# Hybrid decoder layer on one core: a different interleaving of block transposes, LayerNorm passes and sums at the start of the second FFN

## The reference, cut to what matters

```python
def trunk_layer(x, ...):
    x = layer_norm(ALPHA * x + 0.5 * swiglu(x, ffn_wi[0], ffn_wo[0]), ln_g[0], ln_b[0])
    ...                      # attention and retention, merged
    x = layer_norm(ALPHA * x + merged @ w_o, ln_g[1], ln_b[1])
    x = layer_norm(ALPHA * x + 0.5 * swiglu(x, ffn_wi[1], ffn_wo[1]), ln_g[2], ln_b[2])

def swiglu(x, wi, wo):
    g, u = jnp.split(x @ wi, 2, axis=-1)
    return (jax.nn.silu(g) * u) @ wo
```

## Time and profile before

| | |
|---|---|
| median of 3 runs | 2407.12 us (2403.64 to 2409.01) |
| the profiled execution | 2408.45 us, its span 2406.6 us |
| TensorE busy | 2375.1 us (99% of the span) |
| VectorE, ScalarE, GpSimd busy | 1673.8, 911.1, 211.9 us |
| mean granted TensorE clock | 0.996 |

### The profile page before, as it was taken

One profiled execution on the slowest core, in us unless ns is written; L12 is line 12 of the kernel. 1 busy time (PEld: TensorE's weight loads), 2 busy tenths in 40 slices (PEclk: granted clock), 3 DMA queues, 4 the chain that ended last, 5 costly groups with the idle time before them and its releaser, 6 DMA issues.

```text
span 2406.6 us, 30847 instructions
## 1 busy us (share of the span) xinstructions
PE 2375.1 (99%) x12129; PEld 2022.3 (84%) x12129; DVE 1673.8 (70%) x2341; ACT 911.1 (38%) x1347; POOL 211.9 (9%) x297
## 2 busy tenths in 40 slices
PE   8999999999999999999999999999999999999997
PEld 7888888887888998989999878888788888888886
DVE  8666666657887657666666777578766666665788
ACT  5222222243444337443346333274322222234343
POOL 4000000000111000000100111203300000000011
PEclk9999999999999999999999999999999999999999
DMA  5222223275444334243342445534232222227643
GB/s 166 94 100 97 101 88 110 84 239 198 150 142 120 118 97 119 97 132 104 107 119 88 145 134 168 169 100 155 70 106 74 92 101 97 101 97 232 201 149 127
DMA packets 227855, 300.02 MB, mean 125 GB/s; under 512 B 14464, under 2 KB 167344, under 8 KB 224880
## 3 DMA queue, kind: packets, MB, share of 16 engines
q1 hardware_dynamic: 213392, 239.91, 32.1%
q0 software_dynamic: 13056, 56.48, 6.4%
q10 hardware_dynamic: 1264, 1.67, 0.2%
HBM read 243.81 MB, written 55.18 MB: 124 GB/s over the span
## 4 chain that ended last, share of the span: by engine, by line
PE 91%; DVE 5%; ACT 1%; DMA 1%; issue 1%; POOL 1%; SPq 0%; DVEq 0%; POOLq 0%; ACTq 0%
PE ps L2237 26%; PE ps L2239 26%; PE ps L2238 26%; PE ps L2356 3%; PE ps L2445 1%; PE ps L2446 1%; PE ps L2621 1%; PE ps L2756 1%; PE ps L2733 1%; PE ps L2633 1%; PE ps L2743 0%; DVE b_lo L1565 0%; PE ps L2604 0%; DVE y L1431 0%; DVE h_lo L1564 0%
## 5 line engine op out<-in xcount | busy, mean ns | idle before, releaser
L2237 PE MATMUL ps<-xc_hi,u_both 128*128 128x512 f32 x1240 | 486.7, 392 | 8.0 <-DVE u_both L1623 6.6
L2239 PE MATMUL ps<-xc_hi,u_both 128*128 128x512 f32 x1240 | 484.1, 390 | 0.0
L2238 PE MATMUL ps<-xc_lo,u_both 128*128 128x512 f32 x1240 | 484.0, 390 | 0.0
L520 DVE TENSOR_TENSOR w_lo<-raw,w_hi 128x1024 fp32r<-128x1024 f32 x198 | 238.8, 1221 | 98.2 <-ACT w_hi L514 97.9
L2237 PEld LDWEIGHTS ps<-xc_hi,u_both 128*128 128x128 f32 x1240 | 233.7, 188 | 56.6 <-DVE u_both L1623 6.6
L2239 PEld LDWEIGHTS ps<-xc_hi,u_both 128*128 128x128 f32 x1240 | 233.6, 188 | 49.2
L2238 PEld LDWEIGHTS ps<-xc_lo,u_both 128*128 128x128 f32 x1240 | 233.8, 189 | 48.0
L514 ACT ACTIVATE w_hi<-raw 128x1024 fp32r<-128x1024 f32 x198 | 205.5, 1054 | 160.1 <-PE ps L2239 95.0
L2237 PE MATMUL ps<-b_hi,h_hi 128*128 128x512 f32 x616 | 241.3, 392 | 1.7 <-DVE b_lo L1565 1.6
L2239 PE MATMUL ps<-b_hi,h_lo 128*128 128x512 f32 x616 | 239.8, 389 | 0.0
L2238 PE MATMUL ps<-b_lo,h_hi 128*128 128x512 f32 x616 | 239.7, 389 | 0.0
(11 more groups left out here) (355 smaller groups left out, 4409.5 us busy)
## 6 DMA issues: line engine op xcount, KB each, us to landing
raw<-in_w_in SPq DMA_DIRECT2D x90, 512.0 KB, 3.9
wa<-in_ffn_wi SPq DMA_DIRECT2D x87, 512.0 KB, 3.8
h_raw<-h_spill SPq DMA_DIRECT2D x154, 256.0 KB, 2.8
h_spill<-tm POOLq DMA_DIRECT2D x22, 1024.0 KB, 4.2
b_raw<-in_ffn_wo SPq DMA_DIRECT2D x66, 256.0 KB, 3.7
raw<-in_w_in SPq DMA_DIRECT2D x96, 128.0 KB, 2.6
raw<-in_w_in SPq DMA_DIRECT2D x48, 256.0 KB, 3.1
raw<-in_w_br_ret SPq DMA_DIRECT2D x24, 512.0 KB, 4.3
```

The lines of the kernel that those rows point to most:

```text
L520: nc.vector.tensor_tensor(wslot(n, True), raw[:, s * D:(s + 1) * D], fr(wslot(n, False)), ALU.subtract).then_inc(lo_ready, 1)
L2237: mm(out, a_hi, b_hi, start=first, stop=False)
L2238: mm(out, a_hi, b_lo, start=False, stop=False)
L2239: return mm(out, a_lo, b_hi, start=False, stop=last)
```

## The change

Three pieces of code move; no instruction is added or taken away.

1. In `HEAD` the late blocks of pair 2 move ahead of the second half of product 1.
2. On VectorE the passes of tile 7 move from the queue's front to behind the low parts of pair 1, and the two weight sums move behind the low parts of pair 2.
3. On GpSimd the two passes of tile 8 move in between the sums of pair 2 and of pair 3, and the sums of pair 2 no longer wait for tile 7's passes (those of pair 3 still do).

```diff
-HEAD = (("E", 0), ("E", 1), ("E", 2), ("E", 3), ("U", 0), ("L", 0), ("U", 1), ("L", 1), ("U", 2), ("U", 3), ("L", 2), ("L", 3))
+HEAD = (("E", 0), ("E", 1), ("E", 2), ("E", 3), ("U", 0), ("L", 0), ("U", 1), ("L", 1), ("U", 2), ("L", 2), ("U", 3), ("L", 3))
...
-                if p == 2:
-                    wait_affine(pool, 1, 7)
                 for t in (p, p + 4):
                     wait_affine(pool, 1, t)
...
                     combos(2)
-                    combos(3)
                     pool.wait_ge(ln_rows_mix, 32)
                     pool.wait_ge(ln_hat, hat_count(1, 8))
                     link(nc.gpsimd.tensor_tensor(y_tile(8), y_tile(8), ln_gm[0:SR, :], ALU.mult))
                     nc.gpsimd.tensor_tensor(y_tile(8), y_tile(8), ln_bm[0:SR, :], ALU.add).then_inc(ln_affine, 1)
+                    combos(3)
...
                     affine(1, 6)
-                    affine(1, 7)
                     late(0)
                     w_lo(1, 0, 1)
                     late(1)
+                    affine(1, 7)
+                    late(2)
                     w_sum(1, 0, 0)
-                    late(2)
                     w_lo(1, 0, 2)
                     late(3)
```

## The result

The changed kernel takes 2411.63 us (median of 20 runs; the lowest is 2409.63), against 2407.10 for the kernel before in the same comparison: ratio 1.0021, 95% interval [1.0015, 1.0027]. Predicted was 2411.1 us, from 2405.1 to 2415.0.

What follows compares the result with a forecast made beforehand. TensorE bounds the kernel, with the second FFN's head nearly as much VectorE-bound; +3.8, -0.5, +1.0 and -0.26 start product 2 +4.0 us later, clock 0, so 2407.1 + 4.0 = 2411.1 us, range 2405.1 to 2415.

Steps and rivals of the forecast that it cites:

- weight 1's low part: On VectorE ahead of product 1's first half: takes 1.46 us instead of 1.97, so -0.5 us.
- tile 7's passes: On VectorE behind pair 1's low parts: 6.2 us beside tile 8's GpSimd passes, against 2.39 before, so +3.8 us.
- bare high part of weight 2: ScalarE's high part, formerly under pair 2's low parts, stands bare behind the weight sums: +1.0 us.
- no wait for the sample's tile: Before product 2: the sample's transposes are ready, so it starts 0.06 us behind VectorE's chain, not 0.32: -0.26 us.
- clock, up to the second half: Product 2's first half loses the same 2.4 us to the low clock as before: 0 change.
- The step that failed: Weight 1's low part waits for GpSimd's second sum and ends 1.08 us later, at 1686.03.
- Waits capped at 1.1 us: Rival: tile 7's passes on VectorE take 4.6 us, product 2 starts +1.6 us; chance 0.15.
- The reordering works: Rival: tile 7's passes cost 2.4 us, waits do not grow, GpSimd's queue bounds: -2.0 us; chance 0.12.
- The second fall: Possible clock fall under product 1's second half, costing that half 2.4 us, hidden by pair 3's wait.
- a clock that stays up: Rival: the clock holds through product 2 with the forecast's chain, +1.6 us in all; chance 0.10.
- a longer low clock: Rival: product 2's both halves and the sample products run at the low clock, +6.4 us; chance 0.10.
- The waits of TensorE: Waits of 4.9 us among pair 2's transposes and about 4 us at pair 3's fifth block.

Runs made afterwards that it cites:

- narrow_tile8: The changed kernel with tile 8's two GpSimd passes over 128 of their 1024 columns; ratio to the kernel before 1.0013.
- tile8_last: The changed kernel with tile 8's GpSimd passes back behind pair 3's sums; ratio to the kernel before 1.0013.
- the second's: Second comparison: the changed kernel run again unaltered against the kernel before; 2410.82 us, ratio 1.0030 [1.0018, 1.0042].
- changed_filled: The changed kernel with fourteen spare 128x512 matmuls (4, 8 and 2) where TensorE waits in the second FFN's head; ratio to the kernel before 1.0013.

## Why the prediction was right

**The sum.** Product 2 starts 3.91 us late; the prediction had +4.0. Its terms, each from issue to issue in the timeline above, beside the earlier trace rows:

| term | predicted | measured |
|---|---|---|
| weight 1's low part | -0.5 (1.46 us) | +0.64 (2.61 - 1.97) |
| tile 7's passes | +3.8 (6.2 us) | +2.50 (4.89 - 2.39) |
| bare high part of weight 2 | +1.0 | +1.12 |
| no wait for the sample's tile | -0.26 | -0.27 |
| sum, start of product 2 | +4.0 | +3.99; read directly +3.91 |
| clock, up to the second half | 0 | -0.19 |

The first two terms are each off by more than 1 us and cancel: 7.50 us together, 7.66 predicted. That each was missed and the sum met was not foreseen, but it is not chance alone. GpSimd's queue paces both: its first sum to the end of tile 8's second pass took 11.65 us (1680.92 to 1692.57), and the prediction had 11.76. Since its third sum ran ahead of VectorE's low part, it had begun tile 8's first pass 1.81 us before VectorE came to tile 7, and not 0.45, and VectorE waited so much less for it (a pass of 1.68 us instead of 3.0). That first pass falls inside the band of 1.2 to 2.3 us that the prediction had named as a sign of being wrong; the second, 3.25 us, is the one that bears the forecast out.

**The step that failed** inside the sum is "the weight's low part waits for it [the second sum] and ends 1.08 later". The low part was issued at 1683.09, during the second sum, and yet the third sum ran first (1683.43 to 1684.69). It finished 1.09 us behind that one. The gain on the first half of product 1 was thus 1.75 us against before, not 2.9 (1685.83 stands 6.88 behind tile 6's second pass; before, 8.63).

**Waits capped at 1.1 us** falls: 3.25 us for a pass that takes 1.23 in `narrow_tile8`. The Trainium skill, SBUF — State Buffer, "Who interferes with whom", has a VectorE instruction with two SBUF inputs and a GpSimd instruction that reads SBUF exclude each other for a whole instruction, and the trace agrees: VectorE's passes end 1.09 and 1.08 us behind GpSimd's, GpSimd's second pass 2.20 us behind VectorE's first.

**The reordering works** falls too. Its condition was passes of 2.4 us in sum and no longer waits elsewhere. In `tile8_last` the passes do take that, but the waits elsewhere grow, and product 2 is still 2.61 us late. By parts: TensorE's order alone is worth -0.71 us at the second half, GpSimd's order alone costs +1.19, taking tile 8's passes back out of the changed kernel gains 1.59, putting tile 7's passes back in front loses another 0.4. VectorE's order alone, and the dropped wait for tile 7 alone, were not run; the parts need not add up, since each changes what the others meet.

**The clock** did as forecast. Product 2's first half takes 5.28 us in both kernels (1711.56 - 1706.28; before 1709.06 - 1703.78). The sample products behind it took 1.89 us and not 2.08, so the clock rose a little earlier. The second fall that was held possible, under the second half of product 1, was there and hidden. Windows of TensorE in the changed kernel:

```profile
1694.00:1696.00 2.00, 1.69 (x7) 0.63 0.77 289
1696.00:1698.00 2.00, 2.00 (x6) 0.52 0.45 104
...
1704.00:1706.00 2.00, 1.49 (x12) 0.69 0.00 0
1706.00:1708.00 2.00, 1.72 (x4) 0.50 0.00 0
```

That half took 4.25 us (1694.91 to 1699.16), and TensorE still had to wait 2.81 us at pair 3's fifth block. Neither "a clock that stays up" nor "a longer low clock" came.

**The waits of TensorE** were forecast as 4.9 and about 4 us; they are 3.67 and 2.81, plus 0.76 in front of product 2. The first is shorter because tile 7's passes were (4.89 us and not 6.2). The second is shorter by about what the half product took longer (4.25 us and not 2.86).

**The whole time.** The head explains +3.7 us, 0.15%. The first comparison's interval, from 1.0015, just holds that; the second's begins just above it (1.0018). The medians lie 4.5 and 5.1 us apart. What is more than 3.7 us is not in the head nor behind it (695.35 us against 695.46, so the spills that moved cost nothing there either); no cause for it is known beyond the scatter of the part ahead, and that stays open. That the median came out 0.5 us from the one predicted is thus in part luck. The result lies on the edge between "within 0.2%" and "slower", where the prediction had put 0.66 and 0.29.

## What to carry to other kernels

A full-width VectorE instruction with both inputs in SBUF costs what it meets on GpSimd: read both queues together, and put the end of one behind the end of the other. A wait that keeps two engines apart (here pair 2's sums on tile 7) may be worth its 1.2 us; here taking away a TensorE wait of 1.19 us brought one of 3.67 us, because the work that moved now met longer instructions. Where an effect is smaller than the scatter of whole runs, compare profiles from a fixed point ahead of the edit to one behind it.

## What the runs showed of the hardware

The turn between the two engines is not by order of issue alone. A waiting VectorE instruction let one sum by (2.69 us), the rest of a pass and then a sum (4.45 us) and three sums (4.85 us), against 1.22 us alone. In the 2.69 and 4.85 us cases it got in ahead of the fourth sum, the only one that GpSimd starts with a gap (1684.77 behind an end at 1684.69; the others are issued before the end of the one ahead). But the second weight sum of 4.45 us got in without such a gap, and so did the first weight sum before the change. It ran ahead of the third sum, issued at 1692.57, while the second sum ended at 1692.60:

```profile
1691.32 1.28 POOL L846 TENSOR_TENSOR tm_odd<-y 128x512 f32<-128x512 f32 x1
```

The rule is open.

The clock fell at least once in every head without spare matmuls, each time after a stretch in which TensorE had only transposed or waited. It didn't fall in the kernel before with 11 or 12 of them. In `changed_filled` it fell only just ahead of and under the second half of product 1, ahead of which no spare matmuls stand. A fall cost up to 2.4 us under a half product (5.28 us against 2.86); under the second half of product 1 in the changed kernel it cost nothing at the end, since a wait of 2.81 us followed.
